# A two-layer diffusion backbone on one core: last expert stage, hand-over to the second layer's projection, and one more weight slot

## The reference

```python
for l in range(2):
    hl = modulate(xl, g_attn[l], ...); hc = modulate(xc, g_attn[l], ...)     # RMSNorm, gain, shift and scale
    out_lat, out_ctx = token_mixers(hl, hc, ...)      # (h @ w_in) -> 4 kinds of attention -> concat @ w_out
    xl = xl + gt_a * out_lat
    hl = modulate(xl, g_ffn[l], ...)
    xl = xl + gt_f * expert_choice_ffn(hl, w_router[l], w_gate[l], w_up[l], w_down[l])
    if l == 0:                                        # the context stream ends with the first layer
        xc = xc + cgt_a * out_ctx
        xc = xc + cgt_f * expert_choice_ffn(modulate(xc, ...), ...)
return rmsnorm(xl, g_final)
```

## Time and profile before

| | |
|---|---|
| median of 3 runs | 2238.74 us (2237.46 to 2238.93) |
| profiled execution | 2232.47 us |
| its span | 2230.7 us, mean granted clock of PE 0.967 |
| PE, DVE, ACT, GpSimd busy | 2012.9, 785.7, 501.5, 157.1 us |
| DMA | 515.66 MB, mean 231 GB/s |

### The profile page before, as it was taken

How to read it: one execution, slowest core, us unless ns; L and a number is a source line. 1 busy time by engine, 2 the same in 40 slices (tenths; PEclk the granted TensorE clock), 3 DMA queues, 4 the chain that set the end, 5 groups by cost and what they waited for, 6 DMA issues and landing times. The chain is left out here.

```text
span 2230.7 us, 27197 instructions
## 1 busy us (share of the span) xinstructions
PE 2012.9 (90%) x10622; PEld 962.6 (43%) x10622; DVE 785.7 (35%) x2065; ACT 501.5 (22%) x1174; POOL 157.1 (7%) x155
## 2 busy tenths in 40 slices
PE   5999989999989999999999799889998698887875
PEld 3445455555543332333323556456555233332322
DVE  3322266787761100101001632387776302020203
ACT  3111144454430010000100321254444100000001
POOL 1101000000001001020100101100000000000000
PEclk9999988999999999999999899999999899999998
DMA  9841110000089999999998202100005899999995
GB/s 346 310 141 56 38 38 1 1 1 1 1 326 426 425 384 403 401 374 426 365 409 349 74 19 76 42 35 1 1 1 208 349 427 426 427 426 427 427 426 233
DMA packets 90921, 515.66 MB, mean 231 GB/s; under 512 B 10578, under 2 KB 15612, under 8 KB 36524
## 3 DMA queue, kind: packets, MB, share of 16 engines
q1 hardware_dynamic: 84480, 493.29, 54.4%
q0 software_dynamic: 4416, 15.21, 2.3%
q10 hardware_dynamic: 1900, 5.43, 0.6%
HBM read 498.69 MB, written 15.20 MB: 230 GB/s over the span
## 5 line engine op out<-in xcount | busy, mean ns | idle before, releaser
L662 PE MATMUL psS<-arena 128*64 128x512 f32 (+9 forms) x4544 | 1167.0, 558 | 68.3 <-DMA arena<-in_w_up 28.1
L662 PEld LDWEIGHTS psS<-arena 128*64 128x64 f32 (+4 forms) x4544 | 461.5, 159 | 669.3 <-issue 607.3
L665 PE MATMUL psT<-ident,arena 128*128 128x128 f32 (+2 forms) x936 | 153.3, 292 | 74.8 <-DVE arena L1823 25.5
L1973 DVE TENSOR_TENSOR arena<-arena,psS 128x512 f32<-128x512 f32 x32 | 20.6, 684 | 553.6 <-PE psS L662 553.6
L1164 ACT ACTIVATE arena<-psS 128x128 f32<-128x128 f32 (+5 forms) x150 | 57.2, 411 | 568.8 <-PE psS L662 521.7
L665 PEld LDWEIGHTS psT<-ident,arena 128*128 128x128 f32 (+2 forms) x936 | 110.3, 147 | 161.6 <-issue 104.1
L1164 ACT ACTIVATE arena<-psS,nb 128x768 f32<-128x768 f32 (+2 forms) x200 | 158.9, 794 | 78.7 <-DVE nb L1814 77.2
L662 PE MATMUL psT<-arena 128*32 128x512 f32 x1536 | 174.7, 595 | 0.0
L1809 DVE TENSOR_REDUCE mx<-psS 128x1 f32<-128x768 f32 (+2 forms) x200 | 165.0, 825 | 22.6 <-PE psS L662 21.0
L1164 ACT ACTIVATE arena<-psT 128x512 f32<-128x512 f32 (+4 forms) x211 | 108.5, 516 | 223.8 <-PE psT L665 211.9
L662 PE MATMUL psO<-arena 128*64 128x128 f32 (+2 forms) x1600 | 151.1, 297 | 0.0
(11 more groups left out here) (227 smaller groups left out, 1377.0 us busy)
## 6 DMA issues: line engine op xcount, KB each, us to landing
arena<-in_w_gate SPq DMA_DIRECT2D x116, 1024.0 KB, 20.7
arena<-in_w_up SPq DMA_DIRECT2D x116, 1024.0 KB, 18.5
arena<-in_w_down SPq DMA_DIRECT2D x116, 1024.0 KB, 24.9
arena<-in_w_mod SPq DMA_DIRECT2D x40, 1024.0 KB, 8.0
arena<-in_w_in SPq DMA_DIRECT2D x6, 2048.0 KB, 7.8
gtb<-in_w_mod SPq DMA_DIRECT2D x8, 1024.0 KB, 7.0
arena<-in_w_out SPq DMA_DIRECT2D x8, 512.0 KB, 7.6
arena<-in_w_out SPq DMA_DIRECT2D x2, 2048.0 KB, 14.3
```

Source lines behind the costliest of these rows:

```text
L662: return nc.tensor.matmul(o, lhsT, rhs, start=start, stop=stop)
L665: return nc.tensor.transpose(o, in_, ident[0:n, 0:n])
L1973: last = V.tensor_tensor(ar[:, a:a + 512], ar[:, a:a + 512], bank(2 * g + h), ALU.mult)
```

## The change

It does five things. (1) In the last stage of the last quad of the first layer PE computes the context group first (`last_order`); `combine` waits for `yl` per tile, so the context jobs need the context group alone; DVE does the four context adds between the last `weighted` and its low half. (2) The combination uses banks 6, 7, 4, 5, 0, 1, 2, 3 in turn instead of six banks. (3) The root of the first pair of tiles is begun before the last four adds. (4) The second layer's up-projections are loaded at once, and the first section's weights in two parts: rows 0 to 4 of 8 after the last quad's up stages, rows 5 to 7 after the last low half; the other section still waits for `ffn_done`. In the second layer PE's turns of `EARLY` come after the products of their step, not ahead. (5) `gtb` moves into the arena with its halves exchanged (`gate(n)`), which leaves the place of the context gates to a seventeenth slot of the second layer's ring.

```diff
+WIN_EARLY = 5
+def last_order(l):
+    return (2, 0, 1) if l == 0 else (0, 1)
...
-        AR = 36864
+        AR = 38912
+        gtb = ar[:, AR - 2 * D:AR]
+        def gate(n):
+            a = AR - 2 * D + (n * 512 + D) % (2 * D)
+            return ar[:, a:a + 512]
...
-        RINGS = (FIRST_SLOTS, [(X, 0), (tables, 0)] + ARENA_SLOTS + [(modrow, 0)])
+        RINGS = (FIRST_SLOTS, [(X, 0), (tables, 0)] + ARENA_SLOTS + [(ar, 35840), (modrow, 0)])
-        NSLOT, TILES_AT = (11, 16), (22784, 26624)
+        NSLOT, TILES_AT = (11, 17), (22784, 26624)
...
-        COMBINE_BANKS = ((6, 7), (6, 7, 0, 1, 2, 3))
+        COMBINE_BANKS = ((6, 7), (6, 7, 4, 5, 0, 1, 2, 3))
...
@@ sync: the loads of w_in
+                def section_rows(sec, k0, k1):
+                    _, c0, _, nc_ = SECTIONS[sec]
+                    at = WIN + sec % 2 * 4096
+                    load(ar[:, at + k0 * nc_:at + k1 * nc_].rearrange("p (k n) -> p k n", k=k1 - k0),
+                         A["w_in"][l, k0 * P:k1 * P, c0:c0 + nc_].rearrange("(k p) n -> p k n", p=P), z[f"win{sec % 2}"])
                 if l:
                     up_projections()
-                for sec, (_, c0, _, nc_) in enumerate(SECTIONS):
+                    sp.wait_ge(z["done"], groups_done(l - 1, NQ - 1, 7, 2))
+                    section_rows(0, 0, WIN_EARLY)
+                    sp.wait_ge(z["yl"], split_tile(l - 1, NQ - 1, last_order(l - 1)[-1]))
+                    section_rows(0, WIN_EARLY, KD)
+                    sp.wait_ge(Z[l - 1]["ffn_done"], l)
+                for sec in range(len(SECTIONS)):
...
-                    if l and j == NSLOT[l] - 1:
+                    if l and j == NSLOT[l] - 2:
                         sp.wait_ge(z["fgev"], 4 * L)
...
@@ tensor: the steps of the projection
                 for tau in range(NSTEP + 4):
-                    for t in EARLY.get(tau, ()):
+                    for t in EARLY.get(tau, ()) if l == 0 else ():
                         turned(t)
...
                         last.then_inc(z["proj"], 1)
+                    for t in EARLY.get(tau, ()) if l else ():
+                        turned(t)
...
@@ tensor: combine, and the groups
-                    pe.wait_ge(z["yl"], split_tile(l, q, NX - 1))
                     for n, (t, h) in enumerate(CJ):
                         b = combine_bank(q, n)
                         take(b)
                         groups = [2] if t < TC else [0, 1]
+                        if h == 0:
+                            pe.wait_ge(z["yl"], split_tile(l, q, groups[-1]))
...
-                        for g in range(NX):
+                        for g in last_order(l) if (q, st) == (NQ - 1, NSTAGE - 1) else range(NX):
...
@@ vector
+            def pair_root(z, g):
+                dve.wait_ge(z["sq"], 2 * g + 2)
+                rsqrt_begin(ss[:, 2 * g:2 * g + 2], 2, D)
...
-                    for g in range(NX):
+                    for g in last_order(l) if q == NQ - 1 else range(NX):
                         weighted(q, g)
+                        if q == NQ - 1 and l < L - 1 and g == last_order(l)[-1]:
+                            dve.wait_ge(s_sum, 32)
+                            combined(q, range(2 * TC))
+                        if q in COMBINED[l]:
+                            rest(q, g)
                 if l < L - 1:
-                    dve.wait_ge(s_sum, 32)
-                    combined(NQ - 1)
+                    combined(NQ - 1, range(2 * TC, len(CJ) - 4))
+                    pair_root(Z[l + 1], 0)
+                    combined(NQ - 1, range(len(CJ) - 4, len(CJ)))
```

More of the change, by code:

```diff
@@ L239, in backbone_program @@
         eff = sb("eff", L * 32)
-        gtb = sb("gtb", 2 * D)
         ROPE, WUQ, WUKV, MASK = 0, 576, 1344, 1856
@@ L337, in normed_row @@
             old = view(modrow, 0, P, 0, (1536, 2), (1, 512)) if l == 0 else modrow[:, 0:D]
-            return (ar[:, PB + D:PB + 2 * D], gtb[:, D:2 * D], old, ar[:, OS:OS + D], ar[:, 2048:2048 + D])[i]
+            return (ar[:, PB + D:PB + 2 * D], gtb[:, 0:D], old, ar[:, OS:OS + D], ar[:, 2048:2048 + D])[i]
         tmp = ar[:, TMP:TMP + 256]
@@ L382, in backbone_program @@
         Z = [sems(l, "sq xn ht htev htevd proj pact pdve dsq bsq bt btev bs bsa bsd kn kpe kt "
-                     "S nb P T PTa PTd O mj me gp ge cp ce") for l in range(L)]
-        once = {n: sem(n) for n in "open want gd gt gtev rbp rb fg fgev yh yl wb wo lgev pe_ex prb at dup dupT ffn_done xready fxn_sq fxn xr lp st xt xtd lgp lgpc xp done silu prod hp Cn bn qs he y win0 win1 mixed Og xg".split()}
+                     "S nb P T PTa PTd O mj me gp ge ce") for l in range(L)]
+        once = {n: sem(n) for n in "open want gd gt gtev rbp rb fg fgev yh yl wb wo lgev pe_ex prb at dup dupT ffn_done xready fxn_sq fxn xr lp st xt xtd lgp lgpc xp done silu prod hp Cn bn qs he y win0 win1 mixed Og xg cp".split()}
         for z in Z:
@@ L516, in _ @@
                         sp.wait_ge(z["proj"], (sec - 1) * TT)
-                    at = WIN + sec % 2 * 4096
-                    load(ar[:, at:at + KD * nc_].rearrange("p (k n) -> p k n", k=KD),
-                         A["w_in"][l, :, c0:c0 + nc_].rearrange("(k p) n -> p k n", p=P), z[f"win{sec % 2}"])
+                    if l == 0 or sec:
+                        section_rows(sec, 0, KD)
                     if l == 0 and sec == 0:
@@ L793, in _ @@
                         if t == 0:
[L794 removed]
+                            pe.wait_ge(z[f"win{sec % 2}"], 16 * (l * (4 - 2 * (sec % 2)) + sec // 2 + 1))
                         if tau >= NB:
@@ L1120, in group @@
                         experts, n, col = range(QUAD), CAP_C, 256
+                        for e in experts if (q, st) == (NQ - 1, NSTAGE - 1) else ():
+                            pe.wait_ge(*slot_filled(l, (q * NSTAGE + st) * QUAD + e))
                     for h in range(2):
@@ L1382, in _ @@
                             act.wait_ge(z["gt"], 4 * l + g + 1)
-                            a_(gtb[:, g * 512:(g + 1) * 512], bank((4, 5, 6, 4)[g])).then_inc(z["gtev"], 1)
+                            a_(gate(g), bank((4, 5, 6, 4)[g])).then_inc(z["gtev"], 1)
                     for j in jobs:
@@ L1412, in _ @@
                         act.wait_ge(s_xd, 16 * (l * TT + len(tl)))
-                    a_(gtb[:, n * 512:(n + 1) * 512], bank(n)).then_inc(z["fgev"], 1)
+                    a_(gate(n), bank(n)).then_inc(z["fgev"], 1)
                 for g in range(MOD_FRONT, 3 * L) if l == 0 else ():
@@ L1450, in _ @@
                         modulated(x, 6 + x % 2)
-                    for g in range(NX if q in COMBINED[l] else 0):
-                        act.wait_ge(z["y"], hidden_tile(l, q, g))
+                    for g in (last_order(l) if q == NQ - 1 else range(NX)) if q in COMBINED[l] else ():
+                        act.wait_ge(z["y"], hidden_tile(l, q, last_group(l, q, g)))
                         for h in range(2):
@@ L1586, in _ @@
                 for g in range(PAIRS):
-                    dve.wait_ge(z["sq"], 2 * g + 2)
-                    rsqrt_begin(ss[:, 2 * g:2 * g + 2], 2, D)
+                    if not l or g:
+                        pair_root(z, g)
                     if l and g:
@@ L1722, in job @@
                         b = 6 if i == len(tiles) - 1 and r else 7
-                        g = (0 if t >= TC else 1) * D + r * 512
-                        link(V.tensor_tensor(bank(b), bank(b), gtb[:, g:g + 512], ALU.mult))
+                        link(V.tensor_tensor(bank(b), bank(b), gate((0 if t >= TC else 2) + r), ALU.mult))
                         x = t * D + r * 512
@@ L1982, in weighted @@
                 def weighted(q, g):
-                    dve.wait_ge(z["done"], groups_done(l, q, 11, g))
+                    dve.wait_ge(z["done"], groups_done(l, q, 11, last_group(l, q, g)))
                     c = q + 8 if g == 2 else q * 2 + g
@@ L1986, in weighted, with rest @@
                         a = HID + g * D + h * 512
-                        m = (D if g == 2 else 0) + h * 512
-                        last = V.scalar_tensor_tensor(ar[:, a:a + 512], bank(2 * g + h), LG[:, c:c + 1], gtb[:, m:m + 512],
+                        last = V.scalar_tensor_tensor(ar[:, a:a + 512], bank(2 * g + h), LG[:, c:c + 1], gate((2 if g == 2 else 0) + h),
                                                       ALU.mult, ALU.mult)
                     last.then_inc(z["y"], 1)
-                    if q not in COMBINED[l]:
-                        return
+                def rest(q, g):
                     dve.wait_ge(z["yh"], split_tile(l, q, g))
```

9 lines of the change are left out of this document (4 added, 5 removed).

## The result

Timed in turns, the kernel before has a median of 2235.84 us and the changed one 2240.72 us (20 runs each; 2232.93 to 2239.14 against 2235.56 to 2247.78). The ratio is 1.0021, with a 95% interval from 1.0011 to 1.0031: slower by 4.7 us, 2.5 to 6.9. The forecast was +4.0 us (2242.7 from the 2238.74 of the first three runs). It called changes within 4.5 us no change. The interval lies on both sides of that bound, so the measurement doesn't decide between no change and slower in that sense; that the change costs something is clear. The profiled execution of the changed kernel has a span of 2235.4 us against 2230.7.

What follows compares the result with a forecast made beforehand. The prediction took DMA weight loading to bound the second layer's experts and PE's idle time to price the stretch between layers. Terms -1.8 + 4.7 + 3.2 - 2.1 = +4.0 us took 2238.74 to 2242.7; range 2236.0 to 2248.0.

Steps and rivals of the forecast that it cites:

- Context group first: First layer's last combination: context products run early, but DVE's four context adds delay the latent products; net -0.1 us.
- Root between the adds: After the first layer's combination: GpSimd's root for the first pair of tiles runs under the last four adds; -2.1 us.
- Weights in two parts: SP's early load of the first section's weights: three more issues cost nothing and cover the moved projection.
- Up to the first low-rank transpose: Second layer's start, up to PE's wait for the first normalised low-rank row: -1.8 us, bounds -3.0 and 0.
- Turn 5 behind projection 2: Second layer's projection on PE: turn 5 comes later, delaying tile 1's norm and the second low-rank row; +4.7 us.
- Clock: PE at half clock for 3.2 us behind each of two waits over 5 us at the low-rank transposes; +3.2 us.
- Slot: Second layer's weight ring: a seventeenth load uses idle DMA time, -2.46 us, less 0.4 for delayed gathers; -2.1 us.
- the slot does nothing: Rival for the second layer's ring: gathers slip by all of 2.46 us; sum +6.1, 2244.8 us; chance 0.06.
- The rule of alternating queues: At the second layer's first gathers: DMA engines alternate queues packet by packet, so about 1 us is lost; sum 0.6 higher.

Runs made afterwards that it cites:

- sixteen slots: The changed kernel with the second layer's ring put back from 17 slots to 16, `gtb` staying in the arena: 2240.22 us, ratio 1.0018 to the kernel before.
- weights late: The changed kernel with both parts of the first section's weights loaded behind the combination, as before: 2243.89 us, ratio 1.0038 to the kernel before.
- all turns ahead: The changed kernel with all second-layer turns put back ahead of their projections, the rest of the change kept: 2231.01 us, ratio 0.9971 to the kernel before.

## Why the prediction was right, point by point

- *Context group first: -0.1 us.* The added wait is as described, but the products started at 12.71 and not 13.3, mostly since adds back to back take 0.60 us and not 0.69. The last product is 0.15 us later than before, with 5.2 us of half clock in place of 3.2, which the term left out. At equal clock the part is worth about 0.8 us. Small miss of a small term.
- *Root between the adds: -2.1.* From the last add to the rows it is 3.44 us before and 1.42 now, -2.0. Right.
- *Weights in two parts: nothing, and a cover for the moved projection.* Right; without it A is 3.8 us longer, and projection 0 starts 2.3 us later, not 4.
- *Up to the first low-rank transpose: -1.8, bounds -3.0 and 0.* Measured -2.3. The rows give 1.9 of it. The other 0.4 is nearer to full clock, as forecast, but not at the place named: the first turn, behind its shorter wait, still ran at half clock (1.97 us), and what changed is that projection 0 no longer did (2.41 us, not 3.40). The move of projections 0 and 1 took 0.3 us away at the same clock (17.12 us with the turns ahead, 17.38 in the change).
- *Turn 5 behind projection 2: +4.7.* Counted from the first transpose, turn 5 moved from 0.17 to 6.71 us, that is 4.7 and 1.8 of clock, and from turn 5 to the second transpose it is 6.82 us in both kernels, as the chain had it. Shown twice: by undoing it (A -7.0) and by letting ACT and DVE pass it over (A -6.3). Both figures hold the second wait's clock besides the 4.7. The 4.7 by itself shows where both waits are filled: turn 5 comes 4.91 us behind the first transpose, against 0.17 before.
- *Clock: +3.2.* Measured 3.4 by filling both waits. The condition (both waits longer than 4.7 us) was met, and at these two places no unfilled wait of 5.4 us or more was followed by full clock. But the 4.7 us is no bound below which the clock stays up: in the change it fell behind 3.72 us in the combination and behind 2.27 ahead of the first turn.
- *Slot: -2.1.* This term was mis-sized. The load's 2.46 us are there, but the cost of the gathers was set at 0.4; at the first expert product it is 1.8 against the run with sixteen slots (9.99 and 8.21 us) and 1.2 against the kernel before (8.78). B shows 0.2 us for the slot against the former and 1.4 against the latter, and the total none. I had reasoned that the load would be through before the second gather; in fact both gathers were late, the first by 1.9 us and the second by 0.7 to 1.1. The rival "the slot does nothing" described it better than the forecast. The rule of alternating queues of the Trainium skill ("DMA: Bandwidth & Descriptors", queues, rings and completion order), which stood beside the sum as an estimate of about 1 us, was nearer than my 0.4, though still short. No run shows in what order the packets went.

The sum of the terms up to measure A was -1.8 + 4.7 + 3.2 = +6.1; the trace has +6.0, as -2.3, +4.7 and +3.6 (1.8 of clock behind each wait). With the slot at -0.2 in place of -2.1 the forecast for the total would have been +5.9, at the upper side of the interval of 2.5 to 6.9. So the path was right term by term, and the closeness of the total was partly luck.

## What to carry to other kernels

When an engine's order is changed, follow what each moved step releases on the other engines: projection 2 had room to wait, turn 5 had not, since two programs held tile 1's norm behind it. A load put into idle DMA time is free only if no short transfer on the critical path falls into it; let it wait for that transfer. And a wait of some microseconds on PE can be paid twice, by its length and by the clock behind it; products that nobody reads, shorter than the wait, gave the second part back in these runs.

## What the runs showed of the hardware that I had not expected

In section D PE waits 3.2 us at one place in every trace, with the same work around it. The same projection behind it, 16 passes of 128x256, took 3.6 us in four of the fourteen traces (3.62 in the kernel before), 5.0 to 5.3 in seven, and 6.4 to 6.5 in three, the changed kernel among them:

```profile
1410.97 0.48 PE L692 MATMUL psT<-ident,arena 128*128 128x128 f32 x1 [3.19 <-ACTq L1306]
1411.24 6.44 PE L689 MATMUL psS<-arena 128*128 128x256 f32 x16
```

So behind a wait of this length the clock fell in some traces and not in others, and not for equally long. That makes up to 2.9 us at this place, but not in the end: from the end of A to the first gather it is 374.36 us before and 374.53 in the change; in other stretches the changed kernel had the higher clock (for one, 1.00 against 0.83 in the ten microseconds that begin 220 us behind the start of this projection). There is one trace of each kernel, and the three with 6.4 to 6.5 (the change, sixteen slots, weights late) are those with all of the change's order in the projection and nothing filled, so it need not be chance alone.

The plainest case lies in the combination. Nine kernels have a wait of 3.72 or 3.73 us ahead of the latent products, with the same work around it; in eight traces half clock followed, in that of all turns ahead the clock stayed at 1.00. Behind the unfilled wait of 5.4 us ahead of the first low-rank transpose projection 2 took 5.87 to 6.84 us in all five traces that have it. All this may be part of why single executions of one kernel lie some microseconds apart, and why marks in the trace told these versions apart better than totals did. The filled waits kept the clock at 1.00 in every place they were put, the shortest with 1.9 us of filling in waits of 2.6 and 2.3.
